# Pooling mixer of a decoder step in three chunks with its sums of squares on TensorE, and the fourth down piece reordered

## The reference, cut to what matters

```
xn  = rms_norm(x)
g   = 0..3, w = 2, 4, 8, 16, channels 256 g .. 256 g + 255
y_g = (mean of the last w rows of xn_g - xn_g) @ pool_w[g]
x   = x + concat(y_g) * pool_scale
xn  = rms_norm(x)
x   = x + (silu(xn @ w_gate) * (xn @ w_up)) @ w_down
```

## Time and profile before

| what | value |
|---|---|
| median of 3 runs | 2505.83 us (2500.18 to 2505.84) |
| profiled execution | 2498.2 us |
| its span | 2496.2 us |
| mean granted clock of TensorE | 0.972 of full speed |
| busy: PE, DVE, ACT, POOL | 94%, 66%, 38%, 32% |
| chain that ended last | PE 77%, DVE 7%, issue 5%, DMA 3%, ACT 3%, POOL 3% |

### The profile page before, as it was taken

The page is one execution under the profiler, slowest core; times in us unless marked ns, Lnnn a source line. Parts: engine busy times, 40 slices in busy tenths (PEclk is TensorE's granted clock), DMA queues, the critical chain, the costliest instruction groups (busy, mean ns, idle before and its releaser), DMA issues.

```text
span 2496.2 us, 47458 instructions
## 1 busy us (share of the span) xinstructions
PE 2337.5 (94%) x18133; PEld 2151.1 (86%) x18133; DVE 1657.0 (66%) x3482; ACT 942.5 (38%) x2058; POOL 800.8 (32%) x815
## 2 busy tenths in 40 slices
PE   7999998888889979999999899988899999989997
PEld 6778876645568979999999899978899999989997
DVE  4312046555675497878787788748878777778867
ACT  5221133355674243434343222254434343432224
POOL 0020100045433014444443332650344343433335
PEclk9999999999998989999999999987899999999999
DMA  4322379964563023434345765312233434385742
GB/s 168 110 80 77 116 274 403 386 200 127 168 202 102 18 89 114 177 114 176 115 172 187 292 236 208 114 29 89 83 146 138 153 126 165 114 329 203 276 140 106
DMA packets 175088, 406.98 MB, mean 163 GB/s; under 512 B 9507, under 2 KB 111220, under 8 KB 165915
## 3 DMA queue, kind: packets, MB, share of 16 engines
q1 hardware_dynamic: 135283, 191.66, 22.4%
q10 hardware_dynamic: 33792, 164.90, 16.7%
q0 software_dynamic: 5808, 47.64, 5.5%
HBM read 299.37 MB, written 138.31 MB: 175 GB/s over the span
## 4 chain that ended last, share of the span: by engine, by line
PE 77%; DVE 7%; issue 5%; DMA 3%; ACT 3%; POOL 3%; SPq 2%; ACTq 0%; DVEq 0%; POOLq 0%
PE ps L2584 51%; PE ps L2325 13%; PE ps L2359 2%; PE ps L972 2%; PE ps L956 2%; PE ps L991 1%; DMA kraw<-cache_win_k_a 1%; PE ps L2414 1%; SPq L1082 1%; POOL wsum L1307 1%; POOL x L1328 1%; DMA wraw<-w_out 1%; DVE wc L2009 1%; ACT sm L860 1%; POOL wcf L1307 1%
## 5 line engine op out<-in xcount | busy, mean ns | idle before, releaser
L2584 PE MATMUL ps<-xnr,wc 128*128 128x272 f32 x6336 | 845.3, 292 | 38.4 <-issue 17.9
L2584 PEld LDWEIGHTS ps<-xnr,wc 128*128 128x128 f32 x6336 | 824.9, 192 | 41.6 <-issue 23.8
L2584 PE MATMUL ps<-x2b,wc 128*128 128x272 f32 x2376 | 317.2, 290 | 8.7 <-DVE x L2108 5.2
L2584 PE MATMUL ps<-x2a,wc 128*128 128x272 f32 x2376 | 316.8, 290 | 7.1 <-DVE ot L2054 2.8
L2584 PEld LDWEIGHTS ps<-x2b,wc 128*128 128x128 f32 x2376 | 306.2, 190 | 12.2 <-DVE x L2108 5.3
L2584 PEld LDWEIGHTS ps<-x2a,wc 128*128 128x128 f32 x2376 | 305.8, 189 | 10.2 <-issue 6.8
L2325 PE MATMUL ps<-wp,xn 128*128 128x512 f32 (+1 forms) x1080 | 245.4, 389 | 0.0
L2325 PEld LDWEIGHTS ps<-wp,xn 128*128 128x128 f32 (+1 forms) x1080 | 196.3, 182 | 48.9
L1307 POOL TENSOR_TENSOR wsum<-wr 128x512 f32<-128x512 f32 (+2 forms) x87 | 102.5, 1178 | 405.3 <-DMA wr<-w_up 170.1
L2009 DVE TENSOR_TENSOR wc<-wr,wc 128x512 fp32r<-128x512 f32 (+2 forms) x261 | 208.1, 797 | 5.3 <-ACT wc L1560 5.0
L1269 POOL TENSOR_TENSOR sm<-sm,pstat 128x128 f32<-128x128 f32 (+7 forms) x96 | 108.8, 1147 | 317.3 <-DVE pstat L733 317.3
(11 more groups left out here) (277 smaller groups left out, 3298.8 us busy)
## 6 DMA issues: line engine op xcount, KB each, us to landing
hidden<-stg ACTq DMA_DIRECT2D x40, 1904.0 KB, 6.6
xnr<-hidden ACTq DMA_DIRECT2D x40, 1088.0 KB, 9.6
wr<-w_up SPq DMA_DIRECT2D x22, 1024.0 KB, 5.4
wr<-w_gate SPq DMA_DIRECT2D x21, 1024.0 KB, 5.5
kraw<-cache_win_k_a SPq DMA_DIRECT2D x8, 2048.0 KB, 14.8
vraw<-cache_win_v_a SPq DMA_DIRECT2D x8, 2048.0 KB, 11.7
kraw<-cache_k_b SPq DMA_DIRECT2D x64, 256.0 KB, 5.7
vraw<-cache_v_b SPq DMA_DIRECT2D x64, 256.0 KB, 11.1
```

The costliest lines, as they stand in the source:

```text
L2584: r = mm(out, wc[:, q, a, kt * P:(kt + 1) * P], slot(moving_at(u, kt), q, b_), start=(q < 4 and kt == 0 and i == 0), stop=(kt == n - 1 and ...
```

## The change

Two things. The order of the fifth down piece is given to the fourth as well (from unit `UNIT_S`), with its six weight sets. And the mixer runs in three chunks of 384, 256 and 448 columns; `band` products run one chunk ahead of the groups; a square is no longer folded on DVE but summed on PE, one matmul by ones for each of the eight tiles, accumulated in PSUM; group results rotate over banks 0 to 2; `row_scale` comes one tile later on ACT; root and reciprocal of the last chunk come ahead of unit 0's parts instead of inside it.

```diff
-CH = {..., 3: ((0, 384), (384, 256), (640, 256), (896, 192))}
-ROWS = ((0, 3), (3, 5), (5, 7), (7, 9))
+CH = {..., 3: ((0, 384), (384, 256), (640, 448))}
+ROWS = ((0, 3), (3, 5), (5, 9))
...
-        SETS = UNIT_Z // 2 + 6
+        UNIT_S, SET_S = UNIT_Z - 8, UNIT_Z // 2 - 4
+        SETS = SET_S + 12
...
         def set_at(u):
-            return u // 2 if u < UNIT_Z else UNIT_Z // 2 + LAST_SET[u - UNIT_Z]
+            if u < UNIT_S:
+                return u // 2
+            p, r = divmod(u - UNIT_S, 8)
+            return SET_S + 6 * p + LAST_SET[r]
...
+            p, r = divmod(u - UNIT_A, 8)
+            return ("down", p) + (LAST_DP[r] if u >= UNIT_S else divmod(r, 2))
...
-            return UNIT_A + 8 * p + 6 + tp if p < LASTP else UNIT_T - 1 + 2 * tp
+            return UNIT_A + 8 * p + (6 + tp if p < LASTP - 1 else 5 + 2 * tp)
...
+        def pool_bank(c, k):
+            return (KD * c + k) % 3
+
+        def pool_sum_bank(c):
+            return 4 if c == 2 else 3
...
-                    sp.wait_ge(group_done, ADD0[1 + 2 * layer] + 24)
+                    sp.wait_ge(group_done, ADD0[1 + 2 * layer] + (8 if layer else 24))
```

On ACT:

```diff
+            def pool_square(c, k):
+                c0, cn = CH[3][c]
+                act.wait_ge(group_added, POOL_A + KD * c + k + 1)
+                if k >= 2:
+                    act.wait_ge(squares_added, FD0[3] + 7 * c + k - 1)
...
+                act.activation(psq[:, k % 2, 0:cn], x[:, k, c0:c0 + cn], ACT.Square).then_inc(squares_ready, 1)
...
                     row_square(4 + k // 2)
-                    row_scale(4 + k // 2)
-                if k == 3:
+                    if k > 1:
+                        row_scale(3 + k // 2)
+                if k == 5:
                     hi(POOL_U, 0, wpool)
             row_square(8)
+            row_scale(7)
             row_scale(8)
             for k in range(KD):
-                chunk_square(3, 0, k)
+                pooled_high(1, k)
             for k in range(KD):
-                pooled_high(1, k)
...
+                pool_square(0, k)
+            pool_root(0)
             for k in range(KD):
                 pooled_high(2, k)
...
+                pool_square(1, k)
+            pool_root(1)
+            norm_high(1, 0, V11)
+            for k in range(KD):
+                pool_square(2, k)
...
```

On DVE, from the second chunk on (the folds and the fourth chunk are gone):

```diff
+            for c in range(2):
+                for k in range(KD):
+                    pool_add(c, k)
             for k in range(KD):
                 pooled_low(2, k)
+                if k == 2:
+                    chunk_recip(3, 0)
+                if k == 4:
                     norm_quarter(1, 0, 0, 0)
+            chunk_recip(3, 1)
             for k in range(KD):
                 pool_add(2, k)
+                if k == 1:
+                    norm_quarter(1, 0, 0, 1)
+                if k == 3:
                     norm_sum(1, 0, V1)
+                if k == 5:
                     norm_quarter(1, 0, 1, 1)
+            norm_sum(1, 0, V2)
             norm_low(1, 0, V11)
+            set_low(1, 0, 0)
+            norm_quarter(1, 0, 1, 0)
+            norm_sum(1, 0, V3)
+            norm_sum(1, 0, V4)
+            for q in range(1, PARTS):
                 norm_low(1, 0, NORM_LO[q])
                 set_low(1, 0, q)
+            chunk_recip(3, 2)
             ffn_dve(1)
```

On PE:

```diff
+            def square_sum(c, k):
+                pe.wait_ge(squares_ready, SQ0[3] + KD * c + k + 1)
...
+                mm(ps[:, pool_sum_bank(c), 0:cn], ones[:], psq[:, k % 2, 0:cn], start=k == 0,
+                   stop=k == KD - 1).then_inc(squares_summed if k == KD - 1 else squares_added, 1)
...
-            for c in range(NC):
-                if c:
-                    for k in range(KD):
-                        band(c, k)
-                        if k == 3:
-                            pe.wait_ge(rows_scaled, 9)
-                            chunk_sum(3, c - 1)
-                for kt in range(KD):
-                    pool_group(c, kt)
+            for k in range(KD):
+                band(1, k)
+            for kt in range(KD):
+                pool_group(0, kt)
+            for kt in range(KD):
+                pool_group(1, kt)
+                square_sum(0, kt)
+            for k in range(KD):
+                band(2, k)
+                square_sum(1, k)
+            for kt in range(KD):
+                pool_group(2, kt)
+                if kt >= 3:
+                    square_sum(2, kt - 3)
+            for k in range(5, KD):
+                square_sum(2, k)
             ffn(1)
```

More of the change, by code:

```diff
@@ L1190, in ffn_sp @@
                 set_load(layer, 0)
-                sp.wait_ge(group_added, ADD_PER * (layer + 1))
+                sp.wait_ge(group_added, ADD_END[layer])
                 sp.dma_start(x_kept[:], x[:]).then_inc(x_stored, 16)
@@ L1661, in chunk_square, with pool_root @@
                                ACT.Square).then_inc(squares_ready, 1)
+            def pool_root(c):
+                c0, cn = CH[3][c]
+                act.wait_ge(squares_summed, RT0[3] + c + 1)
+                act.activation(prstd[:, c0:c0 + cn], ps[:, pool_sum_bank(c), 0:cn], ACT.Sqrt, bias=small[:, 8:9],
+                               scale=1.0 / D).then_inc(roots_ready, 1)
+            def pool_square(c, k):
+                c0, cn = CH[3][c]
+                act.wait_ge(group_added, POOL_A + KD * c + k + 1)
+                if k >= 2:
+                    act.wait_ge(squares_added, FD0[3] + 7 * c + k - 1)
+                elif c and k == 0:
+                    act.wait_ge(squares_added, FD0[3] + 7 * c)
+                elif c:
+                    act.wait_ge(squares_summed, RT0[3] + c)
+                act.activation(psq[:, k % 2, 0:cn], x[:, k, c0:c0 + cn], ACT.Square).then_inc(squares_ready, 1)
             def row_square(i):
@@ L1777, in _ @@
+            norm_high(1, 0, V2)
+            set_high(1, 0, 2)
+            norm_high(1, 0, V3)
+            set_high(1, 0, 3)
+            norm_high(1, 0, V4)
+            for q in range(4, PARTS):
+                set_high(1, 0, q)
             ffn_act(1)
@@ L1971, in norm_quarter @@
                 q = {(0, 0): V11, (1, 0): V21, (1, 1): V22}.get((row, col))
-                dve.wait_ge(rstd_ready, RT0[r] + 2 * tp + col + 1)
+                dve.wait_ge(rstd_ready, RT0[r] + (min(2 * tp + col, 2) if layer else 2 * tp + col) + 1)
                 for kt in range(4):
@@ L2026, in _, with add @@
             head_recip(dve, 1)
-            def add(a, idx, k, c, scale=None):
+            def add(a, bank, k, c, scale=None):
                 c0, cn = CH[1 if scale is None else 3][c]
@@ L2127, in ffn_dve @@
                                 hidden(layer, u, ("h12", "h21")[q - 5])
-                        if u == 0 and q == 1:
-                            chunk_recip(1 + 2 * layer, NC - 1)
+                        if layer == 0 and u == 0 and q == 1:
+                            chunk_recip(1, NC - 1)
                         if u == 0 and q == 2:
@@ L2178, in _ @@
                 c, k = divmod(idx, KD)
-                add(idx, idx, k, c)
+                add(idx, 4 + idx % 4, k, c)
                 if idx == 1:
@@ L2561, in unit @@
                         pe.wait_ge(set_lo, PARTS * set_number(layer, w) + q + 1)
+                    if layer and u == 0 and q < 3:
+                        pe.wait_ge(group_added, ADD_END[1] - 2 + q)
                     if u < 2:
@@ L2586, in unit @@
                     r.then_inc(part_done, 1)
-                    if u == 0 and q == 0:
-                        chunk_sum(1 + 2 * layer, NC - 1)
+                    if layer == 0 and u == 0 and q == 0:
+                        chunk_sum(1, NC - 1)
             def x_final(layer, i):
```

148 lines of the change are left out of this document (40 added, 108 removed).

## The result

The changed kernel takes 2548.49 us (median of four, 2543.23 to 2552.15) where the kernel before took 2503.40 in the same session: ratio 1.0179, 95% interval 1.0156 to 1.0203, **slower by 45 us**. The forecast was 2522, rival A 2542. The profiled execution took 2547.8 us, span 2546.0, mean granted clock 0.962 (before 0.972).

A forecast was written before the change was run, and what follows sets the result against it. TensorE was named the bound, with DVE also busy in the mixer. Mixer terms 2.6 + 1.5 + 6.1 + 3.9 = 14.1, part 1 at 0 and 2 for weight loads, on 2505.8, gave 2522 us; range 2502 to 2544.

The forecast's parts named there:

- rival A: Third chunk's bands: clock falls to half, 17 us more there and 3 on the groups behind, 2542 us; chance 0.30.
- part 1: Fourth down piece reordered: slot wait goes, weight waits and DVE lag cost as much; 0 us, bounds -5 and +4 a layer.
- 28.1 us at full clock: Third chunk's bands with the second chunk's sums and eight PE waits of 0.99 us for ACT's copy and square.
- Rows, +2.6 and +1.5: Mixer's rows: later row scales make PE wait before tiles 6 to 8, +2.6 us; low clock for some matmuls, +1.5.
- The DVE lag of 2.5: Fourth down piece: DVE falls behind PE over five units that prepare weight sets, 2.5 us taken from 2 to 4.
- the weight wait: Fifth piece's first two parts: PE waits for late-loaded weights, about 2.2 us, and another 1.3 for POOL's sums.
- the clock loss at the fifth piece's start: Head of the last down piece: half-clock start costs 1.5 and 2.6 us in the two layers, within entry costs that could go.
- Tail, +3.9: Mixer after the last group: DVE's list takes 49.1 us against 45.2, +3.9, bounds -4 and +8.
- PE's chain: Mixer up to the last group: PE's list at full clock with eight waits, 71.0 us against 64.9, +6.1.
- B: Mixer: DVE, not PE, sets the pace, so removing 13.6 us of folds pays about 14, 2492 us; chance 0.10.
- C: Both parts cancel: slot wait goes without a new one (-10), mixer costs 14, 2510 us; chance 0.20.
- The list of what to look for: Signs on PE: eight gaps, gaps before tiles 6 to 8, last group about 1738, part-5 wait, fifth-piece weight waits, granted clock.

The follow-up runs named there:

- e3: Changed kernel with each sum of the second chunk one band later on PE, so the eight waits go: 2526.02 us, ratio 1.0093 to the kernel before.
- e1: Kernel before with only the fourth down piece in the order of the fifth and six weight sets, old mixer: 2514.03 us, ratio 1.0044.
- e6: Changed kernel with e3's and e4's edits, pooling weights split where they were before, PE's wait for them behind the second chunk's bands: 2518.78 us, ratio 1.0067.
- e4: Changed kernel with ACT's row scales back in their old place, each right behind its square: 2530.00 us, ratio 1.0122.
- e10: e6 with the eight waits back, each sum right behind its band: 2544.78 us, ratio 1.0168 to the kernel before.
- e7: Changed kernel with second-chunk sums two to a band behind the third chunk's first four bands, first half's norm moved forward: 2520.63 us, ratio 1.0067.
- e12: e8 with each band of the second chunk behind a group of the first: 2507.17 us, ratio 1.0021 to the kernel before.
- e8: e6 in the old piece order, first two chunks' sums inside their own groups, norm spread more evenly: 2504.06 us, ratio 0.9999 to the kernel before.

## Why the prediction was wrong

By the ratios, of 1.79% the waits behind the bands are 0.86 (e3), part 1 0.44 (e1), the rows 0.26 (e6 against e3, not clear of noise): 22, 11 and 6.5 us. The 0.23% left, 6 us, are a remainder that no run isolates; e6's trace has 137.0 us for the mixer as it then is against 131.9, the longer tail among them.

**The clock in the third chunk's bands, rival A at 0.30: this is the step that failed.** The forecast took 28.1 us at full clock, and the execution of e4 whose clock held shows that its price was right (1706.21 to 1734.08, 27.9 us; eight waits of 0.94 are 7.5, forecast 7.9). But the likely case was the fall: in 18 of 21 executions with these waits it came, and the traced one of the changed kernel took 42.9 us. The prediction gave the fall less weight because the bands at 1692 had held the clock after a wait as long; one wait there, eight in a row here. Rival A's 17 and 3 us for it were about the right size: 14.8 in the bands beyond the forecast, and 2.2 in the first 24 group matmuls behind (7.23 instead of e4's 5.03). That A's 2542 came within 6.5 us of the result is partly luck: it has nothing for part 1, 9.7 us too little for the rows and 4.4 for the tail, and these carried the time past the upper end of the range, 2544; but it also starts from 2505.8 and adds 2, where the kernel before took 2503.40 in the session. The Trainium skill (TensorE: Matmul & The Clock Gate, "A second HAM failure mode: psum-queue depth-cycling") says that frequent small pauses between groups of matmuls make the clock swing between its two levels. The traces of the changed kernel and of e10 agree in so far as the clock fell at such pauses, but it did not swing: it stayed at 0.50 for 36 us. e4's trace, at 1.00 through the same pauses, does not agree.

**Rows, +2.6 and +1.5: right in kind, too small.** The forecast's waits before tiles 6, 7 and 8 (1.6, 1.6, 3.0) are 1.67, 0.45 and 3.00 in the changed kernel's trace and 1.67, 1.67 and 3.01 in e3's, which has the same rows. Their price is the clock again: 42.6 us (e3 36.4) against 32.9 forecast, because bands between and behind them ran at half, in the changed kernel all of them from tile 6 on. The +1.5 for "some matmuls" should have been 5 to 11.

**Part 1, 0 us with bounds of -5 and +4 a layer: +11 by e1 (7.5 to 14.5), above the upper bound of 8 in all; in the traces +8.3.** The DVE lag of 2.5 was right: the three units before the stall are 0.5, 1.1 and 1.1 us longer than 5.28. What failed is the place of the weight wait. The prediction put it at the head of the fifth piece, 2.2 + 1.3 us, on PE. It comes one unit earlier, because DVE works in order: the difference for the next set is queued ahead of the adds of the unit that still runs. That unit takes 12.9 us instead of 5.3, so 7.6 where the prediction had 3.5. And the clock loss at the fifth piece's start, 1.5 and 2.6 us and counted as gained, stayed in part: its first unit takes 8.65 us in layer 0 and 8.89 in layer 1 where its second takes 7.91.

**Tail, +3.9: +8.3.** The list on DVE was right up to the reciprocal. Behind it three terms were missing, together some 3 of the 4.4 us: one sum takes 2.37 instead of 1.2 (so did the one at 1760 before), there is a fifth unit add, and a weight difference that takes 1.43 stands ahead of the last unit's second add.

```profile
1807.55 2.37 DVE L2010 TENSOR_TENSOR xnrf<-x2fb,ot 128x1088 f32<-128x1088 f32 x1
...
1816.33 1.43 DVE L2031 TENSOR_TENSOR wc<-wr,wc 128x512 fp32r<-128x512 f32 x1
```

**PE's chain** of groups came out at 21.0 and 15.1 against 21.2 and 14.7, but by two errors: a sum among group matmuls takes PE 0.35 to 0.40 from start to start, not 0.73 to 0.83, and four sums stand ahead of the last group, not five; matmuls at half clock at the head of both stretches took that back. At full clock e6 has 19.2 and 13.2.

**Of the rivals,** B fell with the changed kernel's trace: DVE is 22% busy in the bands that now set the pace. C fell with e1. The list of what to look for was right on the eight waits, the gaps before tiles 6 to 8, the part-5 wait, and the clock in the third chunk's bands as the sign that tells A from the forecast; it was wrong on the waits at the fifth piece and on the end of the last group (about 1738, measured 1768).

## What to carry to other kernels

A short wait on PE must be priced with the clock that it may cost, not by its own length: eight waits of 0.94 us cost 25 us, and a reordering of PE's list (each sum one band later) took them away. When a weight set is made ready later, look for what stands behind its preparation on the in-order engine that does it: the stall appears in the unit before, not in the one that uses the weights. And work taken off an engine that waits for another need not gain anything: the folds left DVE, and the tail grew by 8 us. Only where the rest of DVE's list was moved forward into the time that became free did the tail fall (e7: 42 us), and a part came back as waits for late adds.

## What the runs showed of the hardware

Two things were unexpected. The clock can stay at half while PE never idles: 25.00 of 25.00 us busy at 0.50 in e12, on turns and bands, and 14.00 of 14.00 in e8 on bands; in e6 the same bands were back at full clock 1.5 us after they began, behind a wait of 3.08. And the same eight waits left it at full in the traced execution of e4 and at half in four other traces; by time and mean clock it was three executions at full and 18 at half. So a stage with such waits has two times, 15 us apart, and one trace shows one of them.
